# Expert weights in 1,024-column blocks: gate, up and down products of a top-2 mixture of experts issued by pairs of rounds

## What is computed

```python
D_FF_EXPERT = 7 * D_MODEL // 2          # 3584

def swiglu(xn, w_gu, w_down):
    g, u = jnp.split(xn @ w_gu, 2, axis=-1)
    return (jax.nn.silu(g) * u) @ w_down

def moe_swiglu(xn, router, w_gu, w_down):
    logits = (xn @ router).astype(jnp.float32)
    top_v, top_i = lax.top_k(logits, TOP_K)
    w = jax.nn.softmax(top_v, axis=-1)
    comb = jnp.sum(jax.nn.one_hot(top_i, N_EXPERTS, dtype=jnp.float32) * w[..., None],
                   axis=-2).astype(xn.dtype)
    out = jnp.zeros_like(xn)
    for e in range(N_EXPERTS):
        out = out + comb[..., e:e + 1] * swiglu(xn, w_gu[e], w_down[e])
    return out
```

## Time and profile before

| | |
|---|---|
| median of 3 runs | 2468.37 us (2464.0, 2468.37, 2470.91) |
| profiled execution, device time | 2463.42 us |
| its span | 2461.6 us |
| experts' stage in it, first gate matmul to last down | about 663 to 1668 us |
| PE busy in that stretch of 1005 us | 1000.5 us |
| DVE, ACT busy there | 864.6, 713.8 us |
| mean share of the 16 DMA engines there | 0.96, 348 GB/s |

### The profile page before, as it was taken

How to read it: one execution, slowest core, us unless ns; L and a number is a source line. 1 busy time by engine, 2 the same in 40 slices (tenths; PEclk the granted TensorE clock), 3 DMA queues, 4 the chain that set the end, 5 groups by cost and what they waited for, 6 DMA issues and landing times.

```text
span 2461.6 us, 33628 instructions
## 1 busy us (share of the span) xinstructions
PE 2375.8 (97%) x14432; PEld 2118.3 (86%) x14432; DVE 1803.4 (73%) x1834; ACT 1376.9 (56%) x1354; POOL 133.0 (5%) x106
## 2 busy tenths in 40 slices
PE   5999999999899999999999999998998999998999
PEld 5999999789788888888888888876888999888999
DVE  5656566776488888888888888886676676655766
ACT  4345444464477777767677677776454444544433
POOL 2001000001000000000000000004210001301000
PEclk9999999999799999999999999999998999988999
DMA  6653546453299999999999999995333655332553
GB/s 191 204 184 124 172 161 210 135 188 120 85 374 347 350 347 354 346 348 357 344 348 345 353 357 347 355 352 164 103 120 103 205 172 179 112 103 70 192 185 103
DMA packets 309643, 566.90 MB, mean 230 GB/s; under 512 B 12338, under 2 KB 137553, under 8 KB 309360
## 3 DMA queue, kind: packets, MB, share of 16 engines
q1 hardware_dynamic: 305792, 560.39, 65.4%
q10 hardware_dynamic: 3696, 4.30, 0.5%
HBM read 563.60 MB, written 1.05 MB: 229 GB/s over the span
## 4 chain that ended last, share of the span: by engine, by line
PE 85%; DVE 6%; ACT 4%; DMA 3%; POOL 1%; issue 1%; ACTq 0%; DVEq 0%; SPq 0%; POOLq 0%
PE bank L947 21%; PE bank L782 15%; PE bank L965 10%; PE bank L637 9%; PE bank L766 7%; PE bank L625 6%; PE bank L250 5%; DMA raw<-in_od_moe_gu 3%; DVE wL L202 3%; PE bank L1271 3%; PE bank L647 2%; ACT wH L231 2%; PE bank L1220 2%; PE bank L613 2%; DVE arena L202 1%
## 5 line engine op out<-in xcount | busy, mean ns | idle before, releaser
L202 DVE TENSOR_TENSOR wL<-raw,wH 128x2048 fp32r<-128x2048 f32 (+2 forms) x541 | 1212.5, 2249 | 379.8 <-ACT wH L231 377.4
L231 ACT ACTIVATE wH<-raw 128x2048 fp32r<-128x2048 f32 (+2 forms) x541 | 1014.4, 1877 | 555.0 <-PE bank L782 102.7
L947 PE MATMUL bank<-wH,ra 128*128 128x512 f32 x1792 | 579.4, 394 | 2.7 <-DVE wL L202 2.5
L947 PEld LDWEIGHTS bank<-wH,ra 128*128 128x128 f32 x1792 | 337.5, 188 | 75.4 <-issue 3.4
L782 PE MATMUL bank<-ra,wH 128*128 128x256 f32 x2112 | 382.5, 283 | 0.0
L947 PE MATMUL bank<-wL,ra 128*128 128x512 f32 x896 | 349.4, 390 | 0.0
L782 PEld LDWEIGHTS bank<-ra,wH 128*128 128x128 f32 x2112 | 329.7, 192 | 1.1 <-issue 0.8
L782 PE MATMUL bank<-ra,wL 128*128 128x256 f32 x1056 | 298.8, 283 | 0.0
L965 PE MATMUL bank<-wH,ra 128*128 128x512 f32 x896 | 287.0, 391 | 1.8 <-DVE ra L202 1.8
L637 PE MATMUL bank<-wH,ra 128*128 128x512 f32 (+2 forms) x832 | 235.7, 365 | 4.6 <-DVE ra L205 4.6
L782 PEld LDWEIGHTS bank<-ra,wL 128*128 128x128 f32 x1056 | 202.7, 192 | 0.0
(11 more groups left out here) (194 smaller groups left out, 2619.1 us busy)
## 6 DMA issues: line engine op xcount, KB each, us to landing
raw<-in_od_moe_gu SPq DMA_DIRECT2D x224, 1024.0 KB, 6.5
raw<-in_od_moe_down SPq DMA_DIRECT2D x112, 1024.0 KB, 6.7
raw<-in_ev_ffn_gu SPq DMA_DIRECT2D x22, 1024.0 KB, 5.2
raw<-in_ffn_w_gate SPq DMA_DIRECT2D x22, 1024.0 KB, 5.6
raw<-in_ffn_w_up SPq DMA_DIRECT2D x22, 1024.0 KB, 5.4
raw<-in_ffn_w_down SPq DMA_DIRECT2D x22, 1024.0 KB, 5.0
raw<-in_xa_wkv SPq DMA_DIRECT2D x16, 1024.0 KB, 5.2
raw<-in_od_pw_w SPq DMA_DIRECT2D x12, 1024.0 KB, 5.1
```

The costliest lines, as they stand in the source:

```text
L202: self.op.tensor_tensor(out, a, b, op).then_inc(*self.sig.up(name))
L231: self.op.activation(out, a, ACT.Copy, **kw).then_inc(*self.sig.up(name))
L947: m = p.op.matmul(out[:, :], a, b, start=half == 0 and c == 0 and i == 0, stop=half == 1 and c == 3 and i == 2)
```

## The change

The 7 rounds of an expert are taken in four units, three of two rounds and one of the last round alone. In a unit of two, a gate or up block is 256 rows by 1,024 columns (2 chunks of 128 rows, runs of 4 KB) and feeds six matmuls of each of the two rounds; there are four such blocks for gate and four for up. A down block holds the same 256 rows of the weight as before, but two successive rows on each partition, one run of 8 KB; the transposes take every second column of the hidden values to match. Each engine's loop goes over units: gate of unit q, transposes of the rounds of unit q - 1, up of unit q, down of the rounds of unit q - 1. Numbers of blocks, matmuls, transposes, splits and bytes are the same.

```diff
+UNITS = ((0, 1), (2, 3), (4, 5), (6,))
+NU = len(UNITS)
...
-        def moe_gu(e, f, which):
-            col0 = (FE if which == "up" else 0) + f * 512
-            for half in range(2):
-                rect(("moe", e, f, which, half), gu_w[e][half * 512:(half + 1) * 512, col0:col0 + 512], 512, 4)
+        def moe_gu(e, u, which):
+            n = len(UNITS[u])
+            rows, col0 = 512 // n, (FE if which == "up" else 0) + UNITS[u][0] * 512
+            for k in range(2 * n):
+                rect(("moe", e, u, which, k), gu_w[e][k * rows:(k + 1) * rows, col0:col0 + 512 * n], 512 * n, 4 // n)
...
-                rect(("moe", e, f, "down", half), dn_w[e][at:at + 256, :], 1024, 2)
+                put(("moe", e, f, "down", half), [(lambda b: b[:, 0:2048], dn_w[e][at:at + 256, :].rearrange("(p c) n -> p (c n)", c=2))], 2048)
...
-            if 0 < q <= NE * NRD:
-                h = q - 1
+            for h in last:
                 p.wait_ge(*self.dve.of(("htm", h)))
                 self.pe_turn(p, ("hturn", h), [(slice(None), slice(x * 128, (x + 1) * 128)) for x in range(4)],
-                             [self.htm[:, h % 2, x * 128:(x + 1) * 128] for x in range(4)], 128, self.dve, ("hv_lo", h))
+                             [self.htm[:, h % 2, 256 * (x // 2) + x % 2:256 * (x // 2) + 256:2] for x in range(4)], 128,
+                             self.dve, ("hv_lo", h))
...
+    def unit_rounds(self, q):
+
+        return [q // NU * NRD + f for f in UNITS[q % NU]] if 0 <= q < NE * NU else []
...
+        for k in range(2 * n):
+            tag = ("moe", e, u, which, k)
+            wh, wl = self.pe_block(p, tag, 4 // n)
+            first, last = k == 0, k == 2 * n - 1
+            for i, h in enumerate(rounds):
+                ns = slice(512 * i, 512 * i + 512)
+                for c in range(4 // n):
+                    xh, xl = (x[:, 4 // n * k + c] for x in gx)
+                    for j, (a, b) in enumerate(passes(xh, xl, wh[:, c, ns], wl[:, c, ns])):
+                        m = p.op.matmul(outs[i][:, :], a, b, start=first and c == 0 and j == 0, stop=last and c == 4 // n - 1 and j == 2)
```

More of the change, by code:

```diff
@@ L915, in pe_moe @@
         self.pe_gather(p, 0)
[L916 to L919, removed]
-            if 0 < q <= NE * NRD:
-                h = q - 1
+        for q in range(NE * NU + 2):
+            e, u = divmod(q, NU)
+            last = self.unit_rounds(q - 1)
+            if q < NE * NU:
+                self.pe_project(p, e, u, "gate", self.act)
+            for h in last:
                 p.wait_ge(*self.dve.of(("htm", h)))
@@ new lines, in pe_project @@
+    def pe_project(self, p, e, u, which, sig):
+        rounds = self.unit_rounds(e * NU + u)
+        n = len(rounds)
+        outs = [self.bank(p, (which, h), sig, ("gs" if which == "gate" else "htm", h)) for h in rounds]
+        gx = self.picked(e)
+        for g in range(2):
+            for c0 in (0, 4):
+                p.wait_ge(*(self.act, self.dve)[g].of(("gather", e, g, c0)))
+        for k in range(2 * n):
[8 more added lines that the diff above has]
+                        m = p.op.matmul(outs[i][:, :], a, b, start=first and c == 0 and j == 0, stop=last and c == 4 // n - 1 and j == 2)
+                done = ([(which, h)] if last else []) + ([("block", self.index[tag])] if i == n - 1 else [])
+                if done:
+                    m.then_inc(*self.pe.up(*done))
@@ L1605, in act_moe @@
         self.act_gather(a, 0)
[L1606 to L1616, removed]
+        for q in range(NE * NU + 2):
+            e, u = divmod(q, NU)
+            last = self.unit_rounds(q - 1)
+            if q < NE * NU:
+                for k in range(2 * len(UNITS[u])):
+                    self.act_blocks(a, ("moe", e, u, "gate", k))
+                for h in self.unit_rounds(q):
+                    if h > 1:
+                        a.wait_ge(*self.dve.of(("htm", h - 2)))
+                    a.wait_ge(*self.pe.of(("gate", h)))
+                    a.do(("gs", h), self.gs[:, h % 2, :], self.ps(("gate", h))[:, :], ACT.Silu)
+            for h in last:
                 hv = self.pair(8704 + 1024 * (h % 2), 4, 128)
@@ L1621, in act_moe @@
                 a.cp(("hv_hi", h), hv[0], self.ps(("hturn", h))[:, :].rearrange("p (c s) -> p c s", c=4))
[L1622 to L1626, removed]
+            if q < NE * NU:
+                for k in range(2 * len(UNITS[u])):
+                    self.act_blocks(a, ("moe", e, u, "up", k))
+            for h in last:
+                pe_, pf = divmod(h, NRD)
                 for half in range(2):
@@ L2367, in dve_moe @@
         self.dve_gather(v, 0)
[L2368 to L2374, removed]
+        for q in range(NE * NU + 2):
+            e, u = divmod(q, NU)
+            last = self.unit_rounds(q - 1)
+            if q < NE * NU:
+                for k in range(2 * len(UNITS[u])):
+                    self.dve_blocks(v, ("moe", e, u, "gate", k))
+            for h in last:
                 hv = self.pair(8704 + 1024 * (h % 2), 4, 128)
@@ L2378, in dve_moe @@
                      hv[0].bitcast(F32), ALU.subtract)
[L2379 to L2388, removed]
+            if q < NE * NU:
+                for k in range(2 * len(UNITS[u])):
+                    self.dve_blocks(v, ("moe", e, u, "up", k))
+                for h in self.unit_rounds(q):
+                    if h > 1:
+                        v.wait_ge(*self.pe.of(("hturn", h - 2)))
+                    v.wait_ge(*self.act.of(("gs", h)))
+                    v.wait_ge(*self.pe.of(("up", h)))
+                    v.tt(("htm", h), self.htm[:, h % 2, :], self.gs[:, h % 2, :], self.ps(("up", h))[:, :], ALU.mult)
+            if q > NU and q % NU == 1:
+                pe_ = q // NU - 1
                 for n in range(8):
```

53 lines of the change are left out of this document (20 added, 33 removed).

## The result

| | before | after |
|---|---|---|
| median (20 runs each) | 2467.74 us | 2474.07 us |
| lowest to highest | 2462.25 to 2478.42 | 2469.38 to 2482.74 |
| ratio, 95% interval | | 1.0023 [1.0012, 1.0033] |
| profiled execution | 2463.42 us | 2472.25 us |
| its span | 2461.6 us | 2470.5 us |

The forecast was 2460.5 us with a range from 2454 to 2472. The changed kernel is 6.3 us slower by the medians, 2 us above the range and on the wrong side.

The account below looks back on a forecast made before the run. PE was taken to bound the kernel, with DMA engines almost full in the experts' stage. From 2468.37 us, 5.4 (late landings 5.9 less 0.5 for pairs) and 2.5 (half the spread) came off: 2460.5 us, range 2454 to 2472.

Parts of the forecast that it names:

- What bounds the kernel: Experts' stage: PE sets the end, DMA engines nearly full at 0.96; late weights cost PE 5.9 us.
- The releases of the slots: Raw slots in the experts' stage: released up to 0.7 us later once a unit, covered by four slots and faster landing.
- second rival: VectorE's split behind the second htm comes late, PE waits in all 24 units: 19 us, 2485 us; chance 0.08.
- first rival: Weight transfers: wider rows bring nothing, the late stretches' rate being set elsewhere; 2469 us; chance 0.16.
- Late landings, -5.9 us: Experts' stage: faster landings remove nearly all of PE's waits for late weights, 5.9 us, bounds 0 and 5.9.
- The packets' price: Weight transfers: 16 ns per packet, 189 fewer a block on average, 0.19 us off 2.8 us, 6.8%.
- The lower bound named for it: Packets' gain: possibly nothing, since 375 and 356 GB/s came with equal rows and the estimate compares differently loaded stages.
- The aside that 8 KB rows cut in two: Down blocks: 8 KB rows cut into 4 KB packets would take a third of the packets' gain, forecast unchanged.
- Strided transposes, 0: PE's transposes reading every second fp32: no cost, since the weight load hides; at most 4 us.
- third rival: PE's transposes: strided weight load at a quarter of the pace, 25 us more, 2485 us; chance 0.04.
- Half of the runs' spread: Unprofiled runs: half of the median's 4.95 us above the profiled execution is landing waits, 2.5 us off, bounds 0 and 4.95.
- The margins on VectorE and ScalarE: Splits PE needs next, behind paired short operations: margins about 0.2 and 0.3 us left; 0.5 us for all 24 units.

Follow-up runs that it names:

- The last kernel: Changed kernel with both pairs of short operations pulled apart, down blocks and transposes as before, plus a fifth raw slot; 2460.57 us, 0.9969 of the kernel before.
- The pulled-apart pair of kernels: Short operations of a pair separated by splits: in the changed kernel 2462.99 us, 0.9988; in the pairs' order with old blocks and rows 2460.95 us, 0.9986.

## Why the prediction was wrong, step by step

**What bounds the kernel** held. Late landings cost PE about 6 us, and they can be won. The nearest test is the kernel before with a fifth slot: its six periods are 755.90 - 751.52 = 4.38 us shorter, where the prediction read 4.34, and its time is 3.7 us lower by the medians (1.7 to 6.2 by the interval), though the slot is missing from round 4 of the last expert on, where landings still stand in the chain. The last kernel is 6.4 to 7.6 us below the kernel before, where the forecast was 7.9. So the prize was sized about right and given to a change that doesn't win it. One reading was wrong without harm: of the five periods not each has DMA steps in the chain. The fifth, 1264.87 to 1391.26, is 126.39 us long and has none; that it is late by landings too is suggested only by ScalarE's 22.1 us of waits for them in it.

**The releases of the slots: the step that failed.** The prediction saw that "behind them are queued the releases of the raw slots, each up to 0.7 us later" and closed it with "four slots and the faster landing cover it"; the term was 0.5 us for all of it. It was never worked out, though the rows were there. In order of time, ScalarE and then VectorE of the changed kernel in an undisturbed stretch:

```profile
852.93 1.92 ACT L233 ACTIVATE wH<-raw 128x2048 fp32r<-128x2048 f32 x1 [0.80 <-PE bank L961]
855.65 1.92 ACT L233 ACTIVATE wH<-raw 128x2048 fp32r<-128x2048 f32 x1 [0.80 <-PE bank L961]
```

```profile
857.60 2.29 DVE L204 TENSOR_TENSOR wL<-raw,wH 128x2048 fp32r<-128x2048 f32 x1 [0.43 <-ACT wH L233]
```

The copies of two successive blocks start 2.72 us apart, so that four of them take 10.88 us. From the start of a block's copy (855.65) to the end of its split (857.60 + 2.29) it is 4.24 us, 4.26 with the hand-over to SyncE. That leaves 10.88 - 4.26 = 6.6 us from issue to landing. The landings took a median of 6.5 and 6.7 us in the kernel before and 6.6 and 6.7 in the changed one. Inside a product the ring had no margin for half of its transfers, while the margins that I priced (0.2 and 0.3 us) were those of the split ahead of PE. It is not as bare everywhere: over a whole expert a block comes only every 125.26 / 42 = 2.98 us, and ScalarE waited for 109 of the 336 blocks, not for half (110 in the kernel before). Nor is the time of a landing a constant that can be set against the ring; it fell to 5.3 and 5.6 us when the releases came in time. Into this the pairs put some 0.5 us at the hv copies, and by the prediction's own count 0.6 to 0.7 at the htm, in each of 24 units. What they cost in all is measured, some 9 us (1.0023 to 0.9988); how 0.5 us a place grows to that, through landings that become longer themselves, stays open.

The second rival had the operations and the direction right, but priced them at 19 us and bound them to the split that PE needs next; the loss goes through the slots. The first rival was right that the wider rows bring nothing here and that the waits for landings stay, but it put the time at 2469 us and the reason at the rate.

**Late landings, -5.9 us: not recovered.** The changed kernel's chain has landings in four of its six periods and in the first and the last expert, and ScalarE's waits for gate and up went from 88.6 to 67.8 us, not below 30. The share of the DMA engines in the stage fell from 0.96 to 0.93, where the prediction said 0.90.

**The packets' price: 2.3% instead of 6.8%.** This is the queue row of the changed kernel, 700 to 1640 us, to be set against the first of the earlier trace rows:

```profile
q1 hardware_dynamic: 79235, 328.22, 94.0%
```

940 us x 16 x 0.940 / 328.22 MB is 43.1 ps a byte; before it is 44.1. Packets fell by 43%, time by 2.3%. The pulled-apart pair of kernels on one chip says the same: 93.3% for 331.84 MB with wide rows against 95.7% for 331.81 MB with the old ones, 2.5%. The prediction took the slope between two stages of different load for the price of a packet, and it was not that. The lower bound named for it, "compares two stages of different load", was the better reading. What the 2% bring in time isn't settled: pulled apart, the kernels with wide and with old rows are at 0.9988 and 0.9986, the first with some 2 us of strided transposes; wide gate and up blocks with plain transposes are at 0.9974, but that was another chip, and their six periods are 751.08 us against 751.37 with the old rows. The aside that 8 KB rows cut in two would take a third of the gain was off as well: the down blocks save 14 x 128 of an expert's 7,936 packets, 23%.

The rate that the engines can reach was not the wall. These are windows of 685 to 735 us, of the changed kernel and of the same with the pairs apart:

```profile
685.00:735.00 50.00, 50.00 (x224) 40.80 (x223) 44.37 (x27) 35.52 (x24) 0.00 (x0) 1.00 0.98 358
```

```profile
685.00:735.00 50.00, 50.00 (x229) 41.70 (x228) 45.14 (x27) 36.26 (x25) 0.00 (x0) 1.00 1.01 382
```

The same weights by the same packets come at 382 GB/s where the slots are free in time. The kernel before has 377 GB/s in this window, and 392 with the fifth slot, both with the old rows. DMA: Bandwidth & Descriptors of the Trainium skill (Specifications) gives about 358 GB/s as the limit of one core; 382 over 50 us goes past it, in a launch on one core alone, so it is no reason for the missing gain.

**Strided transposes, 0: they cost 2 us.** The weight load went from 139 to 206 ns, half as long again, and the pitch of the four from 0.11 to 0.12 us: 0.03 us a set, 56 sets, 1.7 us; by the periods 125.49 - 125.18 = 0.31 for 7 sets, 2.5 us in 8 experts. The prediction's bound of 4 us held it; the value taken, "the likelier end because the load already hides", was wrong. A load of 139 ns was already longer than the 0.11 us from one transpose to the next, so no row had shown that a longer one would hide; of the 67 ns more, 10 reach the pace of the transposes, and where the others go isn't shown. SBUF — State Buffer of the Trainium skill (Specifications) asks for two hits in a 16-byte line for full bandwidth. By that rule this read would be free; the trace does not agree for a stationary operand of fp32 with a step of 8 bytes. The third rival's quarter of the pace did not occur.

**Half of the runs' spread: not shown.** The last kernel varies between 2456.48 and 2461.95 us in 6 runs, that before between 2459.4 and 2471.68 in 29. But the changed kernel with five slots, which has 1.9 us of landing waits in all, still varies between 2460.47 and 2469.14 in 11 runs, and with the pairs apart it is 2457.2 to 2466.92 in 12; and the time outside the stage moves by 3 us. By these ranges landings are no more than a part of the spread. The term of 2.5 us is not seen in the nearest test either: the kernel before with five slots gained 3.7 us where the two terms, 5.9 and 2.5, promise 8.4.

**The margins on VectorE and ScalarE** for PE's next block held, as the changed kernel with five slots shows. So the 0.5 us that I put there was no underestimate for these splits; what was missing was the account for the slots.

## What to carry to other kernels

A ring of buffers has a margin like any wait: the time of its slots at the pace of the consumer, less copy and release, against the time from issue to landing. Work it out before moving short operations in front of a release; here 6.6 us stood against a median of 6.6 us, and half a microsecond or so, put in at two places of each unit, cost some 9 us, while one split between two short operations or a fifth slot gave it back. The sum only says where to look: the landings change with the releases. DMA engines that are not at full share, together with waits for landings, were here the sign of slots that come late, and longer rows did not remedy it.

## What the runs showed of the hardware

- Packets of 4 and 8 KB instead of 2 and 4 KB saved 2.3 to 2.5% of the engines' time for a byte, not 6.8%.
- The time from issue to landing of 1 MB isn't fixed: 6.6 us (gate and up) and 6.7 (down) at the median with the short operations in bursts, 5.3 and 5.6 us with them apart, for the same packets.
- Over 50 us these transfers reach 382 GB/s with all 16 engines at full share, and 392 with five slots, with rows of 2 and 4 KB.
- A 128-column fp32 weight load from every second element takes 204 to 206 ns instead of 139 to 140, and a row of transposes fed by such loads goes at 0.12 us each instead of 0.11.
